# Mixture-of-experts stage: weighted rows added into a copy of X by the scatter, experts in an order across the groups

## What is computed

```python
x = layernorm(ALPHA * x + mix, ln1_g, ln1_b)
x = layernorm(ALPHA * x + hier_moe(x), ln2_g, ln2_b)

def hier_moe(x):                        # x: 512 tokens of 1024
    gp, gi = top_k(softmax(x @ wg + bg), 1)              # one of 4 groups
    ep, ei = top_k(softmax(expert logits of that group), 2)   # two of its 4 experts
    ep = ep / sum(ep)
    # each token: sum over its two experts of gp * ep * expert(x)
    # expert(x) = (silu(x @ w_gate) * (x @ w_up)) @ w_down,  w_gate, w_up 1024x256, w_down 256x1024
```

## Time and profile before

| what | value |
|---|---|
| median of 3 runs | 2033.45 us (2031.14 to 2034.34) |
| the profiled execution | 2037.82 us, span 2036.1 us |
| busy share of the span | PE 85%, DVE 56%, ACT 44%, POOL 31% |
| expert stage, layer one and two | 412 to 602 us, 1036 to 1228 us of the span |
| scatters, 32, issue to landing | 3.2 to 15.0 us, median 10.7 |
| copies of X to HBM, 8, issue to landing | median 4.0 us |
| queue q0 (POOL's gathers and scatters), 456.4 to 568.4 us | 14.6% of 16 DMA engines' time, 6.05 MB |
| queue q1 (SP's transfers), same stretch | 78.5%, 34.33 MB |

### The profile page before, as it was taken

How to read it: one execution, slowest core, us unless ns; L and a number is a source line. 1 busy time by engine, 2 the same in 40 slices (tenths; PEclk the granted TensorE clock), 3 DMA queues, 4 the chain that set the end, 5 groups by cost and what they waited for, 6 DMA issues and landing times. The chain is left out here.

```text
span 2036.1 us, 22463 instructions
## 1 busy us (share of the span) xinstructions
PE 1723.8 (85%) x7998; PEld 1329.0 (65%) x7998; DVE 1134.5 (56%) x1701; ACT 887.7 (44%) x1326; POOL 637.9 (31%) x338
## 2 busy tenths in 40 slices
PE   5999897769962999997949981998697689999997
PEld 4876634658852876733738861786386578888885
DVE  4926565659956745656459975661655424233242
ACT  3246565248853245666238862223643331111111
POOL 2336623011111335631111110443522124444441
PEclk9999998969986999988969995999698899999998
DMA  5201111179944201021069953320000222222211
GB/s 184 80 32 44 37 47 62 42 294 354 374 180 166 103 32 44 1 83 43 20 270 348 366 211 149 135 76 0 20 1 1 83 103 104 103 84 103 103 62 52
DMA packets 40476, 233.84 MB, mean 115 GB/s; under 512 B 9316, under 2 KB 9700, under 8 KB 20660
## 3 DMA queue, kind: packets, MB, share of 16 engines
q1 hardware_dynamic: 31012, 215.44, 28.2%
q0 software_dynamic: 9216, 16.80, 2.3%
q10 hardware_dynamic: 144, 0.26, 0.1%
HBM read 226.01 MB, written 23.23 MB: 122 GB/s over the span
## 5 line engine op out<-in xcount | busy, mean ns | idle before, releaser
L258 PE MATMUL bank<-XS,WS 128*128 128x512 f32 x864 | 200.3, 394 | 12.1 <-DVE WS L383 10.6
L2360 POOL TENSOR_TENSOR WS<-ring,WS 128x2048 fp32r<-128x2048 f32 x31 | 149.6, 4825 | 188.4 <-ACT WS L2348 188.4
L258 PEld LDWEIGHTS bank<-XS,WS 128*128 128x128 f32 x864 | 164.2, 191 | 47.8 <-DVE WS L383 11.1
L1366 PE MATMUL bank<-WS,XS 128*128 128x512 f32 x768 | 189.8, 404 | 1.1 <-DVE XS L1486 1.1
L2348 ACT CAST WS<-ring 128x2048 fp32r<-128x2048 f32 x31 | 59.3, 1913 | 271.7 <-PE bank L2381 144.0
L2381 PE MATMUL bank<-XS,WS 128*128 128x512 f32 x768 | 174.9, 389 | 3.0 <-DVEq L2410 3.0
L2399 PE MATMUL bank<-WS,US 128*128 128x512 f32 x768 | 174.7, 389 | 0.0
L1366 PEld LDWEIGHTS bank<-WS,XS 128*128 128x128 f32 x768 | 146.5, 194 | 32.5 <-DVE XS L1486 1.9
L2381 PEld LDWEIGHTS bank<-XS,WS 128*128 128x128 f32 x768 | 144.1, 188 | 33.0 <-DVEq L2410 3.2
L2399 PEld LDWEIGHTS bank<-WS,US 128*128 128x128 f32 x768 | 144.2, 188 | 29.9
L1711 PE MATMUL bank<-XS,WS 128*128 128x512 f32 (+1 forms) x600 | 137.8, 392 | 2.9 <-POOLq L1762 2.9
(11 more groups left out here) (505 smaller groups left out, 3458.4 us busy)
## 6 DMA issues: line engine op xcount, KB each, us to landing
raw<-in_w_exp SPq DMA_DIRECT2D x16, 2048.0 KB, 14.2
DN<-in_w_exp SPq DMA_DIRECT2D x32, 1024.0 KB, 9.3
ring<-in_w_ff SPq DMA_DIRECT2D x32, 1024.0 KB, 4.8
raw<-in_w_in SPq DMA_DIRECT2D x20, 1024.0 KB, 4.9
GU<-in_w_exp SPq DMA_DIRECT2D x8, 2048.0 KB, 15.6
XT<-in_w_exp SPq DMA_DIRECT2D x8, 2048.0 KB, 16.0
ring<-in_w_in SPq DMA_DIRECT2D x12, 1024.0 KB, 4.9
raw<-in_w_out SPq DMA_DIRECT2D x8, 1024.0 KB, 4.9
```

Of the source, the lines that this page charges most:

```text
L258: last = pe.matmul(m.ps[g % 8][:, :], WS[:, i % 2, hw, at:at + P], XS[:, hx, k, :], start=(step == 0), stop=(step == 3 * KD - 1))
L1366: last = pe.matmul(m.ps[2 + e % 2][:, :], r.XS[:, e % 2, hx, 4 * half + k, :], r.WS[:, half, hw, k * S:(k + 1) * S], start=(half == 0 and ...
L2360: pool.tensor_tensor(f.WS[:, q % 2, 1, :], f.ring[:, q % 4, :], f.WS[:, q % 2, 0, :].bitcast(F32), ALU.subtract).then_inc(w_low, 1)
```

## The change

The copies of X move from `router` to `norm_stage`, where SP writes each tile, as soon as it is finished, to both `x_rows` and `mixed_rows`; POOL waits for all eight before the first gather. `mixed_rows` has 512 rows now and starts as X. The table holds the token's number and its weight in a high and a low part, so that the weight of each slot stands in a column `WT`. ACT multiplies the expert's result by this column on the way to YE. The scatter adds YE's rows to `mixed_rows` (`compute_op=ALU.add`). Experts are taken in the order 0, 4, 8, 12, 1, 5, ..., so that four in a row are of four groups and share no row; a scatter waits for the one four ahead. `combine_norm` loads 512 KB a tile straight into X and has no additions.

```diff
+ORDER = [4 * (n % 4) + n // 4 for n in range(16)]
...
@@ norm_stage, SP @@
             sp.wait_ge(rows_in, 16)
+            for t in range(NT):
+                sp.wait_ge(finished, t + 1)
+                for dram in (m.rows_dram, m.mixed_dram):
+                    sp.dma_start(dram[t * P:(t + 1) * P, :], m.X[:, t, :]).then_inc(m.rows_out, 16)
@@ norm_stage, finish(t) on DVE @@
-                link(dve.tensor_tensor(m.X[:, t, :], m.X[:, t, :], ln.GB[:, D:2 * D], ALU.add))
+                dve.tensor_tensor(m.X[:, t, :], m.X[:, t, :], ln.GB[:, D:2 * D], ALU.add).then_inc(finished, 1)
@@ router @@
-            for t in range(NT):
-                sp.dma_start(m.rows_dram[t * P:(t + 1) * P, :], m.X[:, t, :]).then_inc(copied, 16)
-            sp.wait_ge(copied, 16 * NT)
...
-            link(dve.tensor_tensor(by_group(r.SEC[:, :, :]), every_group(r.h2[:, :, :]), hot_group, ALU.mult))
-            link(dve.tensor_tensor(r.VAL[:, :, :, 1], m.TOK[:, 1, :].rearrange("p (t a) -> p t a", a=1).to_broadcast([P, NT, NE]), r.SEC[:, :, :], ALU.add))
...
+            link(dve.tensor_tensor(r.h1[:, :, :], r.h1[:, :, :], wide(r.gm[:, :]), ALU.mult))
+            link(dve.tensor_tensor(r.h2[:, :, :], r.h2[:, :, :], wide(r.m2[:, :]), ALU.mult))
+            link(dve.tensor_tensor(r.h1[:, :, :], r.h1[:, :, :], r.h2[:, :, :], ALU.add))
+            link(dve.tensor_tensor(by_group(r.WV[:, :, :]), every_group(r.h1[:, :, :]), hot_group, ALU.mult))
+            link(dve.tensor_copy(r.VAL[:, :, :, 1], r.WV[:, :, :]))
+            link(dve.tensor_tensor(r.VAL[:, :, :, 2], r.WV[:, :, :], r.VAL[:, :, :, 1].bitcast(F32), ALU.subtract))
+            link(dve.tensor_copy(r.VAL[:, :, :, 3], r.VAL[:, :, :, 0].bitcast(F32)))
@@ experts, POOL @@
+                if e >= 4:
+                    pool.wait_ge(ye_out[e % 2], 16 * ((e - 4) // 2 + 1))
-                pool.indirect_dma_start(out=m.mixed_dram, out_offset=bass.IndirectOffsetOnAxis(ap=r.TB[:, e, 1:2], axis=0),
-                                        in_=r.YE[:, e % 2, :], in_offset=None, bounds_check=2 * S - 1, oob_is_err=False).then_inc(ye_out[e % 2], 16)
+                pool.indirect_dma_start(out=m.mixed_dram, out_offset=bass.IndirectOffsetOnAxis(ap=r.TB[:, e, 0:1], axis=0),
+                                        in_=r.YE[:, e % 2, :], in_offset=None, bounds_check=S - 1, oob_is_err=False,
+                                        compute_op=ALU.add).then_inc(ye_out[e % 2], 16)
...
+            pool.wait_ge(m.rows_out, 16 * 2 * NT)
             gather(0)
@@ experts, PE: table_of(e) @@
-                    pe.wait_ge(indexed, e)
+                    pe.wait_ge(weighed, e)
-                    last = pe.matmul(m.ps[7][:, 2 * e:2 * e + 2], r.HOT[:, e % 2, t, :], r.VAL[:, t, e, :], start=(t == 0), stop=(t == NT - 1))
+                    last = pe.matmul(m.ps[7][:, 4 * e:4 * e + 4], r.HOT[:, e % 2, t, :], r.VAL[:, t, ORDER[e], :], start=(t == 0), stop=(t == NT - 1))
@@ experts, ACT: out_home(e) @@
+                act.wait_ge(weighed, e + 1)
-                    act.copy(r.YE[:, e % 2, half * S:(half + 1) * S], m.ps[5 + half][:, :]).then_inc((ye_low, ye_up)[half], 1)
+                    act.mul(r.YE[:, e % 2, half * S:(half + 1) * S], m.ps[5 + half][:, :], r.WT[:, e:e + 1]).then_inc((ye_low, ye_up)[half], 1)
@@ experts, DVE: index(e) @@
-                dve.tensor_scalar(r.TB[:, e, :], m.ps[7][:, 2 * e:2 * e + 2], float(NOWHERE), None, ALU.add).then_inc(indexed, 1)
+                dve.tensor_scalar(r.TB[:, e, :], m.ps[7][:, 4 * e:4 * e + 1], float(NOWHERE), None, ALU.add).then_inc(indexed, 1)
+                dve.reduce_sum(r.WT[:, e:e + 1], m.ps[7][:, 4 * e + 1:4 * e + 3], AX.X).then_inc(weighed, 1)
@@ combine_norm @@
-                sp.dma_start(r.MIX[:, t, :], m.mixed_dram.rearrange("(s c) d -> s (c d)", c=2)[t * P:(t + 1) * P, :]).then_inc(mix_in[t], 16)
+                sp.dma_start(m.X[:, t, :], m.mixed_dram[t * P:(t + 1) * P, :]).then_inc(mix_in[t], 16)
...
-                for c, weight in enumerate((r.gm, r.m2)):
-                    link(dve.scalar_tensor_tensor(out=m.X[:, t, :], in0=r.MIX[:, t, c * D:(c + 1) * D], scalar=weight[:, t:t + 1], in1=m.X[:, t, :], op0=ALU.mult, op1=ALU.add))
```

More of the change, by code:

```diff
@@ L973, in norm_stage @@
     names = ("rows_in", "raw_in", "first_high", "first_low", "w_high", "w_low", "xt_high", "xt_low", "tile_done", "dve_step", "var_ready", "inv_ready", "shift_ready",
-             "standard", "weights_ready", "bias_sum", "turned", "xt_home", "logits", "logits_home", "routed")
+             "standard", "weights_ready", "bias_sum", "turned", "xt_home", "logits", "logits_home", "routed", "finished")
     with stage(nc, "norm_stage", *names) as (block, sems):
         (rows_in, raw_in, first_high, first_low, w_high, w_low, xt_high, xt_low, tile_done, dve_step, var_ready, inv_ready, shift_ready,
-         standard, weights_ready, bias_sum, turned, xt_home, logits, logits_home, routed) = sems
+         standard, weights_ready, bias_sum, turned, xt_home, logits, logits_home, routed, finished) = sems
         at = R_L1
@@ L1175, in router @@
 def router(nc, m, r):
[L1177 to L1181, removed]
-            for t in range(NT):
-                sp.dma_start(m.rows_dram[t * P:(t + 1) * P, :], m.X[:, t, :]).then_inc(copied, 16)
-            sp.wait_ge(copied, 16 * NT)
+    names = ("dve_step", "hot_ready", "rank_done", "total_done", "exp_in", "exp_done")
+    with stage(nc, "router", *names) as (block, (dve_step, hot_ready, rank_done, total_done, exp_in, exp_done)):
         @block.gpsimd
@@ L1281, in experts @@
 def experts(nc, m, r, layer):
-    names = ("hot_row", "table_done", "indexed", "dve_step", "xe_in0", "xe_in1", "ye_out0", "ye_out1", "gu_in0", "gu_in1", "gu_in2", "gu_in3", "dn_in0", "dn_in1", "row_t", "xe_high", "xe_low",
+    names = ("hot_row", "table_done", "indexed", "weighed", "dve_step", "xe_in0", "xe_in1", "ye_out0", "ye_out1", "gu_in0", "gu_in1", "gu_in2", "gu_in3", "dn_in0", "dn_in1", "row_t", "xe_high", "xe_low",
              "w_high", "w_low", "gate_up", "silu_done", "hidden", "ht_done", "ht_high", "ht_low", "down_high", "down_low", "down", "ye_low", "ye_up")
     with stage(nc, "experts", *names) as (block, sems):
-        hot_row, table_done, indexed, dve_step, xe_in0, xe_in1, ye_out0, ye_out1, gu_in0, gu_in1, gu_in2, gu_in3, dn_in0, dn_in1, row_t, xe_high, xe_low, \
+        hot_row, table_done, indexed, weighed, dve_step, xe_in0, xe_in1, ye_out0, ye_out1, gu_in0, gu_in1, gu_in2, gu_in3, dn_in0, dn_in1, row_t, xe_high, xe_low, \
             w_high, w_low, gate_up, silu_done, hidden, ht_done, ht_high, ht_low, down_high, down_low, down, ye_low, ye_up = sems
@@ L1303, in gate_up_in @@
                     sp.wait_ge(w_low, 2 * (e - 3))
-                sp.dma_start(r.GU[e % 4], m.d["w_exp"][bass.ds(layer, 1), e, :, 0:GU].rearrange("a p n -> p (a n)")).then_inc(gu_in[e % 4], 16)
+                sp.dma_start(r.GU[e % 4], m.d["w_exp"][bass.ds(layer, 1), ORDER[e], :, 0:GU].rearrange("a p n -> p (a n)")).then_inc(gu_in[e % 4], 16)
             gate_up_in(0)
@@ L1310, in _ @@
                     sp.wait_ge(down_low, 2 * (e - 1))
-                sp.dma_start(r.DN[:, e % 2, :], m.d["w_exp"][bass.ds(layer, 1), e, :, GU:].rearrange("a p n -> p (a n)")).then_inc(dn_in[e % 2], 16)
+                sp.dma_start(r.DN[:, e % 2, :], m.d["w_exp"][bass.ds(layer, 1), ORDER[e], :, GU:].rearrange("a p n -> p (a n)")).then_inc(dn_in[e % 2], 16)
                 if e + 2 < NE:
@@ L1498, in hot_rows @@
                 for t in range(NT):
-                    dve.tensor_scalar(r.HOT[:, e % 2, t, :], m.IOTA[:, :], r.POS[:, t, e:e + 1], None, ALU.is_equal).then_inc(hot_row, 1)
+                    dve.tensor_scalar(r.HOT[:, e % 2, t, :], m.IOTA[:, :], r.POS[:, t, ORDER[e]:ORDER[e] + 1], None, ALU.is_equal).then_inc(hot_row, 1)
             def index(e):
                 dve.wait_ge(table_done, e + 1)
-                dve.tensor_scalar(r.TB[:, e, :], m.ps[7][:, 2 * e:2 * e + 2], float(NOWHERE), None, ALU.add).then_inc(indexed, 1)
+                dve.tensor_scalar(r.TB[:, e, :], m.ps[7][:, 4 * e:4 * e + 1], float(NOWHERE), None, ALU.add).then_inc(indexed, 1)
+                dve.reduce_sum(r.WT[:, e:e + 1], m.ps[7][:, 4 * e + 1:4 * e + 3], AX.X).then_inc(weighed, 1)
             hot_rows(0)
@@ L1597, in square @@
                 act.wait_ge(finished, t + 1)
-                act.activation(r.MIX[:, t, 0:D], m.X[:, t, :], ACT.Square, accum_out=m.SS[:, t:t + 1]).then_inc(squared, 1)
+                act.activation(r.MIX[:, t, :], m.X[:, t, :], ACT.Square, accum_out=m.SS[:, t:t + 1]).then_inc(squared, 1)
             for t in range(NT):
@@ L2497, in build @@
         m.gate_dram = nc.dram_tensor("gate_rows", (GR, S), F32, kind="Internal").ap()
-        m.mixed_dram = nc.dram_tensor("mixed_rows", (2 * S, D), F32, kind="Internal").ap()
+        m.mixed_dram = nc.dram_tensor("mixed_rows", (S, D), F32, kind="Internal").ap()
         m.d = d
@@ L2505, in build @@
```

(11 more changed lines are left out.)

## The result

| | before | after |
|---|---|---|
| median of the runs | 2033.84 us (6 runs, 2031.14 to 2036.63) | 2051.41 us (6 runs, 2046.46 to 2054.68) |
| profiled execution | 2037.82 us, span 2036.1 | 2049.84 us, span 2048.0 |

The ratio is 1.0084, with a 95% interval of 1.0070 to 1.0099: slower by 0.84%, some 17 us. Terms are compared with the spans, and the verdict is that of the medians.

The account below looks back on a forecast made before the run. Nearly full TensorE, VectorE and DMA bound the expert stage, with transfers at the critical path's edge. Combine -22.2, norm +2.8, router +2.2, adding scatters +28.6 give +11.4 us: 2049.2 profiled, 2044.8 median; range 2015 to 2072.

Parts of the forecast that it names:

- the likeliest case: Whole kernel: an adding row costs near twice a plain one, on half of the engines; 2039 to 2055 us, chance 0.55.
- Half of the engines is full, and the mean hides it: Expert stage: about 8 of 16 DMA engines carry scattered and gathered rows besides weights and are full; mean share 0.93.
- rival of an even spread: Expert stage: rows fall on all 16 engines, whose spare time takes the adds; 2017.6 us, chance 0.12.
- An adding row costs twice a plain one (x = 1): Expert-stage scatters: x is an adding row's extra price over a plain one; 0.33 us a row against 0.165.
- free add: Expert-stage scatters: reading the destination overlaps the rest, x near 0; 2016.3 us, chance 0.17.
- dear one: Expert-stage scatters: an adding row's three passes run in series, x = 2; 2073.4 us, chance 0.16.
- Periods of 11.3 us from the fourth scatter on: Expert stage: gathers pass the allowed 16.4 us and TensorE stalls; periods 11.3 rather than 9.8 us, 13 us a layer.
- The last scatter, +1.3 a layer: End of the expert stage: the last scatter has no cover and lengthens the stage by 1.3 us a layer.
- Combine, -11.1 a layer: combine_norm: two additions leave each tile, 7.9 us, and the second tile comes 3.2 us sooner; 11.1 us less a layer.
- Norm stage, +1.4: End of norm_stage: SP issues two copies of the last tile, 0.72 us each, before the barrier; +1.4 us a layer.
- Router, +1.1: Router, VectorE's chain: two steps go out, three small steps, two more and two casts come in; +1.1 us a layer.
- Engine work and new waits in the expert stage, nothing: Expert stage: added sums, column multiplication, table columns and waits cost nothing; uncovered, +5.4 us in all.

Follow-up runs that it names:

- E1: The changed kernel with the table's slots reordered so that an expert's rows lie on both halves of the 128 partitions; 2021.63 us, ratio 0.9930.
- E2: The kernel before the change with the table's slots reordered so that an expert's rows lie on both halves of the partitions; 2032.53 us, ratio 0.9985.
- E3: The changed kernel with a plain scatter, so that rows are written and not added; 2019.69 us, ratio 0.9921.
- E4: The changed kernel with each scatter waiting for the one right ahead to land, instead of the one four ahead; 2062.97 us, ratio 1.0141.
- E6: E3 with each expert's rows scattered plainly a second time, into a tensor that nothing reads; 2059.44 us, ratio 1.0120.

## Why the prediction was right

The forecast was 2044.8 us, slower, with 2039 to 2055 for the likeliest case; 2051.41 was measured. By its steps:

- **Half of the engines is full, and the mean hides it.** Shown by E1: spreading the rows takes away nearly the whole loss (30 us of 31.7) at an unchanged or higher total load, and E2's last scatter shows the two halves at work. The rival of an even spread falls with it; made true by E1's edit, it gives 2021.6 where it was put at 2017.6.
- **An adding row costs twice a plain one (x = 1).** The busy stretch has 0.18 us more a row, x = 1.1. Over the whole execution q0 goes from 2.3% of 16 engines' 2036.1 us to 3.5% of 2048.0, some 0.19 us more for each of the 2048 adding rows (512 tokens, two experts, two layers), x = 1.2. By E3 the whole term, waits and last scatters with it, is 31.7 to 33 us where the sum had 28.6. The free add (2016.3 us) and the dear one (2073.4) fall. The ratio of 1.93 from the Trainium skill (Collectives: The Full Stack, the section on the bandwidth ceiling), measured there between a copying and a reducing collective, is near: the busy stretch has about 2.0 to 2.1, the lone scatter 0.46 to 0.167, or 2.7.
- **Periods of 11.3 us from the fourth scatter on.** Measured 11.2 to 11.6, and the first wait is that for the gather of 485. The body of layer one's stage grew by 13.2 us (16.1 less 2.9 of the last scatter), against 13; that of layer two's by 10.6 (13.75 less 3.15). Layer two had 3.6 us of such waits already, beside the one at the stage's start, against 0.4 in layer one. The prediction saw that and still gave both layers 13; it is enough for the difference, though no run separates it.
- **The last scatter, +1.3 a layer.** Too small. From its issue to the next stage it is now 7.85 us in layer one and was 4.9: +2.9 (8.03 and 4.88 in layer two). The step counted the rows of the full engines at the busy price. A lone adding row takes 0.46 us, and POOL's own instruction is longer: L1334's mean is 1605 ns, and was 1046. That this term was too small and layer two's body too large is luck for the total: the two expert stages grew by 29.9 us against 28.6.

```profile
L1334 POOL DMA_INDIRECT mixed_rows<-YE,table x32 | 51.4, 1605 | 245.1 <-issue 102.1 <-DVE table L1511 65.9 <-ACT YE L1449 48.6
```

- **Combine, -11.1 a layer.** Measured -10.0. The two additions leave as counted; but the second tile starts 9.3 us after the first issue instead of 11.5, so 2.2 sooner and not 3.2: the megabyte that went was charged at the rate of the last two.
- **Norm stage, +1.4.** Measured +0.75. A pair of issues takes 0.32 and 0.43 us, not 0.72 each: the 0.72 was the mean of four in a row. The barrier waits for SP, as said.
- **Router, +1.1.** Measured +1.24. (The prediction's 0.21 for a small step is 0.20 by its own rows, 0.17 and the gap of 0.03; it changes nothing.)
- **Engine work and new waits in the expert stage, nothing.** E3 agrees. The bound of 0.2 us for ScalarE's multiplication stood on no row; it measured 0.10 (0.69 us a half against 0.59).

The stages sum to 2.4 us more than forecast and the untouched work to 1.9 less, so that the profiled execution comes out at 2049.84 us where 2049.2 was forecast. Nearly all of the 6.6 us between 2044.8 and 2051.41 lies between single profiles and medians: the profile before was 4.4 us above its median and the one after 1.6 below (the runs after spread over 8 us). That the profiles agree to 0.6 us is therefore luck in part.

## What to carry to other kernels

A mean DMA share under 1 can hide engines that are full: landing times that grow at a steady rate of issue show it, and a lone transfer's slices show how many engines it uses. Rows moved by a table belong on partitions spread over both halves; here one line about the order of the slots was worth 30 us, and turned a loss of 0.8% into a gain of 0.7%. An adding scatter takes additions off VectorE, but charge it two passes of its rows on the engines that carry them; where it stood alone at the end of a stage, it cost some 3 us more here.

## What the runs showed that was not expected

- A lone adding row is dearer than one in the busy stretch: 0.46 us against some 0.36, while plain rows take 0.167 alone and 0.18 in the mix.
- The adding form takes POOL longer as an instruction, 1605 ns on the mean against 1027 in E3, with the same table and rows in layer one; the gathers, whose form is unchanged, take longer beside it, too (1237 ns against 1019).
- With all 16 engines at a share of 1.00 (E1) TensorE still waits for nothing in the settled part, and 364 GB/s move instead of 328: a full share is no sign of a bound by itself. Nor is 1.00 a ceiling of this measure, which reads 1.13 from 560.70 to 561.70 us in the change.
- How TensorE's waits are divided matters as much as their sum: eight gaps of 1.3 to 2.7 us left the granted clock at 1.00 (the change), while gaps of 3.74 and 5.64 us were each followed by a stretch at 0.50 (E4). The length of the gap alone doesn't sort these rows: E6 has gaps of 3.26 and 3.30 us with the lower clock behind them, and one of 3.45 at 532.45 with 1.00 before and behind.
